# Two transformer blocks in fp32: another order of work in the first stage, and each head's pipeline step as one burst of TensorE

## The chip, the cores and the metric

One core of one Trainium2 chip runs the whole program. The metric is the device time of one execution in microseconds (us).

## The reference

Everything is fp32. A sequence of 256 tokens with 2048 channels goes through a first block and a second one. What the change touches lies in the first block, up to its attention's output:

```
h = rmsnorm(x, attn_norm)                  # (256, 2048)
proj = h @ w_in                            # (256, 5376)
aq, ak, av, bq, bk, bv, cq, ck, cv = split(proj)
out_a: 8 heads, windowed softmax, sinks, bias table (2 key/value heads)
out_b: 8 heads, stick-breaking: z = q k^T / 8, strictly causal,
       a = exp(log_sigmoid(z) + sum of log_sigmoid(-z) over the keys between)
out_c: 16 heads, softmax over three dilations, bias table
x = x + concat(rmsnorm(out_a), rmsnorm(out_b), rmsnorm(out_c)) @ w_out
```

A feed-forward part with a short convolution follows, then the second block (a pooling layer and a latent attention), which is steered by silu(c) @ ada_w, 12288 columns for each of two layers. Those ada products don't depend on x, and the kernel spreads them over its stages.

## The kernel before, in words

**Weights.** All weights pass through a ring of 4 slots (`raw`, `hi`, `lo`), in chunks of 512 KB: two tiles of 128 rows by 512 columns, or four by 256. SyncE loads a chunk (L943 to L949); it waits until the low half of the chunk four places before is made. ScalarE copies it to fp32r, the high half (`split_hi`, L540), once TensorE has used up the slot's last chunk; VectorE subtracts it from the raw values, the low half (`split_lo`, L544). TensorE multiplies three products (high x high, high x low, low x high), 12 matmuls of 512 columns a chunk (L630 in the first stage). So loads, high halves and low halves run ahead of TensorE by up to four places. An **ada chunk** goes through the same ring but not to TensorE: VectorE multiplies it by the two steering vectors and adds up, 4 instructions (L567, L573). When 8 are summed, TensorE turns the panel (`turn_ada`, L646) and VectorE takes it.

**The first stage** is a loop over c = 0 to 115, written out, that every engine runs in its own order; semaphores tie them. Chunks 0 to 83 are w_in in 11 panels (8 chunks each, panel 6 has 4), chunks 84 to 115 are w_out in 12. At the end of a panel ScalarE takes it out of PSUM (`take_in`, L1126), squares it for the head norms (L1133), VectorE sums the squares (`head_sums`, L1481), and GpSimd makes roots and stages q and k of each head. x itself is turned by TensorE (`turn_x`, L712) and split (`x_high` L725, `x_low` L735) at the start.

**The heads.** 32 heads, 8 "b" (stick-breaking), 8 "c", 8 "a", 8 "c", go through a pipeline of steps, called bursts. `BURST` names the chunk in front of which burst b stands: 19, 22, ... 40; 43, 45, 48, ... 60; 63, 65, ... 77; 79, 80, 82, 84 and so on to 102. At burst b:

- TensorE's `burst(b)`, in front of chunk BURST[b]: turn the mixed tile of two finished heads (L2030), turn q and k of head b (L1968), scores of head b-1 (L1978 to L1982).
- TensorE's `second_burst(b)`, in front of the chunk after it: for head b-3 the turn of the probabilities (L1992) or the stick sum (L2001, L2002), for head b-4 the output (L2019 to L2021). It waits for `exp_done` and `b_soft`, and for `pt_ready` and `b_weights`.
- ScalarE: q and k columns (L1141), the split of weights, then softmax exp (L1168); for every second "b" burst `stick_logs`, abs, exp and ln of a pair of heads (L1181 to L1185, table loads between), behind the weight split. `stick_weights` (L1190) stands at the start of the next chunk.
- VectorE: `soft_turned` and `stick_exponent` and `head_taken` one chunk later, logits and maxima (L1489 to L1500) in the burst's own chunk, then the low halves and ada chunks of that c, and last, one chunk later, `stick_soft` (L1513).

**Other work of the stage.** The position bias is made from 384 distances and a one-hot table (`bias_by_distance`, L1959), stored to DRAM, and read back by 8 transfers of 384 KB with rows of 1 KB (L964), all behind weight chunk 16. `FIRST_ADA` places two ada panels, 16 chunks, behind weight chunks 20, 23, ... 65; a weight or ada chunk is split about 3 to 4 places ahead of its turn. `FIRST_ADA_TURNS` places their turns at 47 and 72, in PSUM bank 7, which the heads' outputs use too, so the turn waits until the outputs are taken. The mean square of x is needed at the end of chunk 7 (`take_in(0)`).

Of the kernel before, what the change touches and what calls it, by code (L numbers as in the profile page):

```python
# [14 lines left out]
P = 128  # L15
# [22 lines left out]
W = 512  # L38
# [65 lines left out]
FIRST_ADA = [20 + 3 * m for m in range(2 * CH)]  # L104
FIRST_ADA_TURNS = [47, 72]
# [194 lines left out]
def two_block_kernel(nc, t, out, consts):  # L300
    ctx = ExitStack()
    with ctx:
# [625 lines left out]
        def _(sp):  # L928
# [30 lines left out]
            for j in range(RING, N_FIRST):  # L959
                load_first(j)  # L960
                if j == 2 * CH:
                    sp.wait_ge(bias_stored, 2 * 16)
                    for p in range(0, P, SHIFTS):
                        sp.dma_start(bias[p:p + SHIFTS, :, :],  # L964
                                     bass.AP(bias_rows.tensor, P - 1 - p, [[3 * P - 1, SHIFTS], [3 * P * SHIFTS, N_TAB], [1, SEQ]]))\
                          .then_inc(bias_loaded, 16)
                for m in range(len(FIRST_ADA)):
                    if first_at(j) + 1 <= FIRST_ORDER.index((True, m)) < first_at(j + 1):
                        c = FIRST_ORDER.index((True, m))
                        load_chunk(sp, c, c % RING, t["ada_w_2"][0][m % CH * CK_T * P:(m % CH + 1) * CK_T * P, m // CH * W:(m // CH + 1) * W], W)  # L970
# [125 lines left out]
        def _(act):  # L1096
# [15 lines left out]
            act.wait_ge(attn_ready, 1)  # L1112
            x_high(act, 0, 0)
            his(act, 0, 0, 0, 0, 2)
            x_high(act, 0, 1)
            his(act, 0, 0, 0, 2, RING)
            x_high(act, 0, 2)
            x_high(act, 0, 3)
# [73 lines left out]
            for c in range(N_FIRST):  # L1192
                for b in bursts_at(c - 1):
                    if headed(b, U_BEHIND, "b"):
                        stick_weights(headed(b, U_BEHIND, "b"))
                for b in bursts_at(c):
                    if b < HEADS:
                        qk_columns(heads[b])
                    if mix_pair(b) is not None:
                        mix_high(mix_pair(b))  # L1200
                if c in X_TURN_AT:
                    x_high(act, 1, X_TURN_AT.index(c))
                his(act, 0, 0, 0, first_at(c) + RING, first_at(c + 1) + RING)
                if c < D // W:
                    act.wait_ge(x_loaded[c], 16)
                    panel_squares(act, 0, c, x_squares[:, :])
# [15 lines left out]
                for b in bursts_at(c):  # L1222
                    if headed(b, S_BEHIND, "ac"):
                        soft_exp(headed(b, S_BEHIND, "ac"))
                    if headed(b, S_BEHIND, "b") and b % 2 == 0:
                        stick_logs(b // 2 - 1)
                    if mix_pair(b) is not None:
                        mix_square(mix_pair(b))
# [212 lines left out]
        def _(dve):  # L1441
# [10 lines left out]
            x_low(dve, 0, 0)  # L1452
            los(dve, 0, 0, 0, 0, 2)
            x_low(dve, 0, 1)
            los(dve, 0, 0, 0, 2, RING)
            x_low(dve, 0, 2)
            x_low(dve, 0, 3)
# [119 lines left out]
            for c in range(N_FIRST):  # L1577
# [3 lines left out]
                for b in bursts_at(c - 1):  # L1581
                    if headed(b, U_BEHIND, "ac"):
                        soft_turned(headed(b, U_BEHIND, "ac"))
                    if headed(b, U_BEHIND, "b"):
                        stick_exponent(headed(b, U_BEHIND, "b"))
                    if headed(b, V_BEHIND, "abc"):
                        head_taken(headed(b, V_BEHIND, "abc"))
                for b in bursts_at(c):
                    if headed(b, S_BEHIND, "ac"):
                        if b == HEADS_B + S_BEHIND:  # L1590
                            dve.wait_ge(bias_loaded, 16 * P // SHIFTS)
                        soft_logits(headed(b, S_BEHIND, "ac"))
                    if headed(b, S_BEHIND, "b"):
                        stick_logits(headed(b, S_BEHIND, "b"))
                    if headed(b, S_BEHIND + 1, "ac"):
                        soft_recip(headed(b, S_BEHIND + 1, "ac"))
                    if mix_pair(b) is not None:
                        mix_low(mix_pair(b))
# [6 lines left out]
                if c == RING:  # L1605
                    vector_columns()
                    x_mean_square(dve, 0)
                if c == CH - 2:
                    bias_rows_ready()
# [6 lines left out]
                for b in bursts_at(c - 1):  # L1616
                    if headed(b, S_BEHIND, "b") and b % 2 == 0:
                        stick_soft(b // 2 - 1)
# [322 lines left out]
        def _(pe):  # L1941
# [62 lines left out]
            def head_out(h):  # L2004
# [3 lines left out]
                for n, at in enumerate(FIRST_ADA_TURNS):  # L2008
                    if BURST[h.n + V_BEHIND] >= at:
# [76 lines left out]
            for c in range(N_FIRST):  # L2086
                if c in (1, 3):
                    pe.wait_ge(x_loaded[(c + 1) // 2], 16)
                    turn_x(pe, 0, (c + 1) // 2)
                if c == RING:  # L2090
                    pe.wait_ge(x_loaded[3], 16)
                    turn_x(pe, 0, 3)
# [4 lines left out]
                for b in bursts_at(c - 1):  # L2097
# [3 lines left out]
                if c in FIRST_ADA_TURNS:  # L2101
                    n = FIRST_ADA_TURNS.index(c)
                    pe.wait_ge(out_taken, sum(BURST[k + V_BEHIND] < c for k in range(HEADS)))
# [309 lines left out]
```

## Time and profile before

| | |
|---|---|
| runs | 2490.86, 2486.44, 2471.79 us; median 2486.44 |
| profiled execution | 2475.26 us, its span 2473.5 |
| TensorE busy | 95% of the span (2348.0 us) |
| VectorE, ScalarE, GpSimd busy | 67%, 42%, 3% |
| DMA | 430.32 MB, mean 174 GB/s |
| mean granted clock of TensorE | 0.98 of full speed |

A row of a timeline gives the start, the duration, the engine, the line of the kernel, the instruction with its operands, and, in brackets, how long its engine was idle before it and what ended that. Matmuls overlap, so what a chunk costs is read from the start of its first matmul to the start of what follows, not from durations. A busy share over the whole span hides that the first stage, until about 478 us, works differently from the rest.

### The profile page before, as it was taken

How to read it: one execution, taken by the hardware profiler on the slowest of the kernel's cores; microseconds unless marked ns; L12 is line 12 of the kernel's file. 1: busy time of each engine (PE TensorE's matmuls, PEld its weight loads, DVE VectorE, ACT ScalarE, POOL GpSimd, SP SyncE). 2: the span in 40 equal slices, each digit the busy share in tenths (PEclk: the TensorE clock that was granted, in tenths of full speed). 3: DMA queues.
4: the chain of work that ended last, by engine and by line, in shares of the span. 5: the costliest groups of instructions: out<-in, count | busy, mean ns of one | idle time of the engine just before them, and what ended most of it. 6: DMA issues, size and time to landing. Idle time of an engine off the chain costs nothing.

```text
span 2473.5 us, 32056 instructions
## 1 busy us (share of the span) xinstructions
PE 2348.0 (95%) x11221; PEld 1944.8 (79%) x11221; DVE 1658.1 (67%) x2401; ACT 1041.2 (42%) x1489; POOL 73.6 (3%) x112
## 2 busy tenths in 40 slices
PE   7889999999999999999979999999899799899998
PEld 6667778878788787777857888888788699799976
DVE  4466757677877877687757665757678666456644
ACT  5455655555555555434343222222322534444333
POOL 1011210000000000000000000000000000000000
PEclk9899999999999999999989999999999899999999
DMA  7855634566766767687754554646566256411243
GB/s 212 202 160 148 178 120 137 173 214 206 235 201 218 228 199 234 217 257 239 249 178 143 160 165 143 197 137 196 188 193 192 85 173 178 130 60 59 81 136 136
DMA packets 225515, 430.32 MB, mean 174 GB/s; under 512 B 13799, under 2 KB 38623, under 8 KB 224128
## 3 DMA queue, kind: packets, MB, share of 16 engines
q1 hardware_dynamic: 222112, 418.96, 54.8%
q10 hardware_dynamic: 2720, 9.83, 1.2%
q8 instruction: 63, 1.03, 0.2%
q14 instruction: 44, 0.36, 0.0%
q0 software_dynamic: 576, 0.14, 0.0%
HBM read 426.16 MB, written 2.72 MB: 173 GB/s over the span
## 4 chain that ended last, share of the span: by engine, by line
PE 61%; issue 19%; DVE 7%; DMA 6%; ACT 5%; SPq 0%; POOL 0%; DVEq 0%; ACTq 0%; POOLq 0%
PE ps L597 35%; PE ps L630 11%; PE ps L607 9%; DMA raw<-in_w_down 4%; DVE lo L544 2%; ACT hi L540 2%; DVE ada_acc L573 2%; PE ps L646 1%; DVE ustage L1633 1%; PE ps L2207 1%; DMA raw<-in_ada_w 1%; DMA raw<-in_w_in 1%; PE ps L2132 0%; SPq L964 0%; PE ps L1982 0%
## 5 line engine op out<-in xcount | busy, mean ns | idle before, releaser
L540 ACT ACTIVATE hi<-raw 128x1024 fp32r<-128x1024 f32 x604 | 634.6, 1059 | 1169.9 <-PE ps L597 528.8
L544 DVE TENSOR_TENSOR lo<-raw,hi 128x1024 fp32r<-128x1024 f32 x604 | 731.8, 1223 | 546.5 <-ACT hi L540 540.3
L573 DVE SCALAR_TENSOR_TENSOR ada_acc<-raw,csil,ada_acc 128x512 f32<-128x512 f32 x720 | 491.8, 748 | 2.7 <-DMA raw<-in_ada_w 2.5
L597 PE MATMUL ps<-hi,h_hi 128*128 128x512 f32 x960 | 383.9, 400 | 8.1 <-DVE lo L544 6.6
L597 PE MATMUL ps<-lo,h_hi 128*128 128x512 f32 x960 | 379.4, 395 | 0.0
L597 PE MATMUL ps<-hi,h_lo 128*128 128x512 f32 x960 | 379.3, 395 | 0.0
L597 PEld LDWEIGHTS ps<-hi,h_hi 128*128 128x128 f32 x960 | 181.2, 189 | 55.7 <-DVE lo L544 13.5
L597 PEld LDWEIGHTS ps<-hi,h_lo 128*128 128x128 f32 x960 | 181.2, 189 | 42.4
L597 PEld LDWEIGHTS ps<-lo,h_hi 128*128 128x128 f32 x960 | 181.3, 189 | 40.2
L630 PE MATMUL ps<-hi,h_hi 128*128 128x512 f32 (+1 forms) x352 | 146.1, 415 | 19.9 <-DVE lo L544 19.9
L597 PE MATMUL ps<-hi,g_hi 128*128 128x512 f32 x352 | 140.9, 400 | 3.0 <-DVE lo L544 2.7
L630 PE MATMUL ps<-lo,h_hi 128*128 128x512 f32 (+1 forms) x352 | 139.7, 397 | 0.0
L597 PE MATMUL ps<-lo,g_hi 128*128 128x512 f32 x352 | 139.6, 397 | 0.0
L597 PE MATMUL ps<-hi,g_lo 128*128 128x512 f32 x352 | 139.4, 396 | 0.0
L630 PE MATMUL ps<-hi,h_lo 128*128 128x512 f32 (+1 forms) x352 | 139.2, 396 | 0.0
L597 PE MATMUL ps<-hi,k_hi 128*128 128x448 f32 (+2 forms) x288 | 102.6, 356 | 1.1 <-DVE k_lo L836 0.6
L597 PE MATMUL ps<-hi,y_hi 128*128 128x512 f32 x256 | 102.5, 400 | 0.0
L630 PEld LDWEIGHTS ps<-hi,h_hi 128*128 128x128 f32 x352 | 69.6, 198 | 41.5 <-issue 15.6
L607 PE MATMUL ps<-h_hi,hi 128*128 128x512 f32 x256 | 102.0, 398 | 0.0
L597 PE MATMUL ps<-hi,y_lo 128*128 128x512 f32 x256 | 101.9, 398 | 0.0
L597 PE MATMUL ps<-lo,y_hi 128*128 128x512 f32 x256 | 101.9, 398 | 0.0
L597 PE MATMUL ps<-hi,k_lo 128*128 128x448 f32 (+2 forms) x288 | 101.5, 353 | 0.0
(319 smaller groups left out, 3751.2 us busy)
## 6 DMA issues: line engine op xcount, KB each, us to landing
raw<-in_ada_w SPq DMA_DIRECT2D x192, 512.0 KB, 4.2
raw<-in_w_up SPq DMA_DIRECT2D x176, 512.0 KB, 4.4
raw<-in_w_down SPq DMA_DIRECT2D x88, 512.0 KB, 5.1
raw<-in_w_in SPq DMA_DIRECT2D x84, 512.0 KB, 4.0
raw<-in_pool_w_in SPq DMA_DIRECT2D x64, 512.0 KB, 4.0
raw<-in_mla_w_in SPq DMA_DIRECT2D x56, 448.0 KB, 4.1
raw<-in_w_out SPq DMA_DIRECT2D x32, 512.0 KB, 3.8
raw<-in_pool_w_out SPq DMA_DIRECT2D x32, 512.0 KB, 4.6
```

What stands on the lines that cost most here:

```text
L540: act.activation(hi[:, slot, :, :], raw[:, slot, :, :], ACT.Copy).then_inc(hi_split, 1 + ada)
L544: dve.tensor_tensor(lo[:, slot, :, :], raw[:, slot, :, :], hi[:, slot, :, :].bitcast(F32), ALU.subtract).then_inc(lo_split, 1)
L573: ins = dve.scalar_tensor_tensor(acc, raw[:, slot, k, :], csil[:, v, kt:kt + 1], acc, ALU.mult, ALU.add)
L597: mm = pe.matmul(ps[:, bank, 0:n], a[:, kt0 + k, tok * P:(tok + 1) * P], w[:, slot, k, col0:col0 + n], start=first and k == 0 and s == 0, ...
L607: mm = pe.matmul(ps[:, bank0 + n, :], w[:, slot, k, n * P:(n + 1) * P], a[:, kt0 + k, :], start=first and k == 0 and s == 0, stop=last and ...
L630: mm = pe.matmul(ps[:, PAIR * half + tok, 0:width], x, w[:, k, :], start=first and k == 0 and s == 0, stop=last and k == nk - 1 and s == 2)
L646: mm = pe.matmul(ps[:, bank, at:at + 1], acc, negones[:, 0:1], start=True, stop=True)
L1633: ins = dve.scalar_tensor_tensor(conv[which][:, m, back:SEQ], turned_u(m)[:, 0:SEQ - back], cols[:, bass.ds(ch + vec[0] * P + vec[1], 1)], ...
L2207: mm = pe.matmul(ps[:, m, s * SEQ + c0:(s + 1) * SEQ], u[:, TT * s + k, m * P:(m + 1) * P], poolm[:, bass.ds(n, 1), k, c0:].rearrange("p a ...
```

## The change

- **One burst.** `second_burst(b)` and VectorE's items of it stand at BURST[b] itself, in front of `burst(b)`, no longer one chunk later. `stick_weights` follows in the same chunk, behind the split of weights.
- **Logs first.** `stick_logs` stands in front of ScalarE's split of weights, `stick_soft` in front of VectorE's logits and splits of the next chunk.
- **The start.** ScalarE does a small activation as soon as its operand is set, then splits weight chunk 0 before x's first part, and so on in turns; VectorE does the same. TensorE turns x panels 1 and 2 in front of chunk 1, panel 3 in front of chunk 2. The squares of x move from chunks 0 to 3 to chunks 2 to 5, its mean from 4 to 6.
- **The bias loads** go one by one behind weight loads 20, 22, ... 34.
- **The ada chunks** go behind weight chunks 40, 42, 45, 47, ... 77, their turns to 62 and 83, and bank 7's order follows.

```diff
--- before.py
+++ after.py
@@ -101,8 +101,9 @@
          + [79 + 23 * k // 12 for k in range(N_BURSTS - 24)])
 QK_READY = {0: IN_AT[2], 8: IN_AT[5], 16: IN_AT[8], 24: IN_AT[10]}
 STAGE_AT = [max(BURST[max(k - PAIR, 0)] if k >= PAIR else 0, QK_READY[k // 8 * 8]) for k in range(HEADS)]
-FIRST_ADA = [20 + 3 * m for m in range(2 * CH)]
-FIRST_ADA_TURNS = [47, 72]
+FIRST_ADA = [40 + 5 * m // 2 for m in range(2 * CH)]
+FIRST_ADA_TURNS = [62, 83]
+BIAS_AT = range(20, 36, 2)
 GROUP_MEAN_AT = [BURST[12] + 1, BURST[28] + 1, BURST[36] + 1]
 X_TURN_AT = [OUT_AT[8 + n + 1] + 1 for n in range(D // W - 1)]
 UP_PAIRS = 2
@@ -958,12 +959,12 @@
             load_x(3)
             for j in range(RING, N_FIRST):
                 load_first(j)
-                if j == 2 * CH:
+                if j in BIAS_AT:
+                    p = BIAS_AT.index(j) * SHIFTS
                     sp.wait_ge(bias_stored, 2 * 16)
-                    for p in range(0, P, SHIFTS):
-                        sp.dma_start(bias[p:p + SHIFTS, :, :],
-                                     bass.AP(bias_rows.tensor, P - 1 - p, [[3 * P - 1, SHIFTS], [3 * P * SHIFTS, N_TAB], [1, SEQ]]))\
-                          .then_inc(bias_loaded, 16)
+                    sp.dma_start(bias[p:p + SHIFTS, :, :],
+                                 bass.AP(bias_rows.tensor, P - 1 - p, [[3 * P - 1, SHIFTS], [3 * P * SHIFTS, N_TAB], [1, SEQ]]))\
+                      .then_inc(bias_loaded, 16)
                 for m in range(len(FIRST_ADA)):
                     if first_at(j) + 1 <= FIRST_ORDER.index((True, m)) < first_at(j + 1):
                         c = FIRST_ORDER.index((True, m))
@@ -1109,13 +1110,13 @@
             act.sem_inc(mla_taken, PAIR)
             for s in (x_squared, u_staged[0], u_staged[1], g_hi_done):
                 act.sem_inc(s, FREE)
-            act.wait_ge(attn_ready, 1)
-            x_high(act, 0, 0)
-            his(act, 0, 0, 0, 0, 2)
-            x_high(act, 0, 1)
-            his(act, 0, 0, 0, 2, RING)
-            x_high(act, 0, 2)
-            x_high(act, 0, 3)
+            act.wait_ge(consts_set, 1)
+            act.activation(x_squares[:, 0:TT], halves[:, 0:TT], ACT.Identity)
+            for n in range(D // W):
+                his(act, 0, 0, 0, n, n + 1)
+                if n == 0:
+                    act.wait_ge(attn_ready, 1)
+                x_high(act, 0, n)
 
             def take_in(p):
 
@@ -1190,20 +1191,22 @@
                 act.activation(stick_one(b_w, h), stick_one(b_z, h), ACT.Exp).then_inc(b_weights, 1)
 
             for c in range(N_FIRST):
-                for b in bursts_at(c - 1):
-                    if headed(b, U_BEHIND, "b"):
-                        stick_weights(headed(b, U_BEHIND, "b"))
                 for b in bursts_at(c):
                     if b < HEADS:
                         qk_columns(heads[b])
                     if mix_pair(b) is not None:
                         mix_high(mix_pair(b))
+                    if headed(b, S_BEHIND, "b") and b % 2 == 0:
+                        stick_logs(b // 2 - 1)
                 if c in X_TURN_AT:
                     x_high(act, 1, X_TURN_AT.index(c))
                 his(act, 0, 0, 0, first_at(c) + RING, first_at(c + 1) + RING)
-                if c < D // W:
-                    act.wait_ge(x_loaded[c], 16)
-                    panel_squares(act, 0, c, x_squares[:, :])
+                for b in bursts_at(c):
+                    if headed(b, U_BEHIND, "b"):
+                        stick_weights(headed(b, U_BEHIND, "b"))
+                if c in range(2, 2 + D // W):
+                    act.wait_ge(x_loaded[c - 2], 16)
+                    panel_squares(act, 0, c - 2, x_squares[:, :])
                 if c == CH - 2:
                     act.wait_ge(ext_ready, 2)
                     for to, e, n in ((0, 0, HEADS_A), (HEADS_A, 1, HEADS_C)):
@@ -1222,8 +1225,6 @@
                 for b in bursts_at(c):
                     if headed(b, S_BEHIND, "ac"):
                         soft_exp(headed(b, S_BEHIND, "ac"))
-                    if headed(b, S_BEHIND, "b") and b % 2 == 0:
-                        stick_logs(b // 2 - 1)
                     if mix_pair(b) is not None:
                         mix_square(mix_pair(b))
                 if c + 1 in X_TURN_AT or c + 1 == N_FIRST:
@@ -1449,12 +1450,9 @@
             dve.memset(table[N_BUCKETS:N_BUCKETS + 1, :], 1.0).then_inc(consts_set, 1)
             dve.wait_ge(attn_turned, 1)
             dve.tensor_copy(attn_col[:, :], ps[:, 0, 0:KT]).then_inc(attn_ready, 1)
-            x_low(dve, 0, 0)
-            los(dve, 0, 0, 0, 0, 2)
-            x_low(dve, 0, 1)
-            los(dve, 0, 0, 0, 2, RING)
-            x_low(dve, 0, 2)
-            x_low(dve, 0, 3)
+            for n in range(D // W):
+                los(dve, 0, 0, 0, n, n + 1)
+                x_low(dve, 0, n)
 
             def vector_columns():
 
@@ -1578,13 +1576,16 @@
                 for p in HSS_OF:
                     if IN_AT[p + 1] == c:
                         head_sums(p)
-                for b in bursts_at(c - 1):
+                for b in bursts_at(c):
                     if headed(b, U_BEHIND, "ac"):
                         soft_turned(headed(b, U_BEHIND, "ac"))
                     if headed(b, U_BEHIND, "b"):
                         stick_exponent(headed(b, U_BEHIND, "b"))
                     if headed(b, V_BEHIND, "abc"):
                         head_taken(headed(b, V_BEHIND, "abc"))
+                for b in bursts_at(c - 1):
+                    if headed(b, S_BEHIND, "b") and b % 2 == 0:
+                        stick_soft(b // 2 - 1)
                 for b in bursts_at(c):
                     if headed(b, S_BEHIND, "ac"):
                         if b == HEADS_B + S_BEHIND:
@@ -1604,8 +1605,8 @@
                     group_mean(GROUP_MEAN_AT.index(c))
                 if c == RING:
                     vector_columns()
+                if c == CH - 2:
                     x_mean_square(dve, 0)
-                if c == CH - 2:
                     bias_rows_ready()
                 if c == FIRST_ADA[0]:
                     dve.wait_ge(c_silu, 1)
@@ -1613,9 +1614,6 @@
                     if OUT_AT[q + 1] == c + 1:
                         add_out(q)
                 los(dve, 0, 0, 0, first_at(c) + RING, first_at(c + 1) + RING)
-                for b in bursts_at(c - 1):
-                    if headed(b, S_BEHIND, "b") and b % 2 == 0:
-                        stick_soft(b // 2 - 1)
 
             def add_panel(done, c, half, col0):
 
@@ -2006,7 +2004,7 @@
                 if h.n:
                     pe.wait_ge(out_taken, h.n)
                 for n, at in enumerate(FIRST_ADA_TURNS):
-                    if BURST[h.n + V_BEHIND] >= at:
+                    if BURST[h.n + V_BEHIND] > at:
                         pe.wait_ge(ada_taken, n + 1 + FREE)
                 pe.wait_ge(proj_taken, h.v_panel + 1)
                 if h.kind == "b":
@@ -2084,23 +2082,21 @@
             pe.wait_ge(x_loaded[0], 16)
             turn_x(pe, 0, 0)
             for c in range(N_FIRST):
-                if c in (1, 3):
-                    pe.wait_ge(x_loaded[(c + 1) // 2], 16)
-                    turn_x(pe, 0, (c + 1) // 2)
+                for n in {1: (1, 2), 2: (3,)}.get(c, ()):
+                    pe.wait_ge(x_loaded[n], 16)
+                    turn_x(pe, 0, n)
                 if c == RING:
-                    pe.wait_ge(x_loaded[3], 16)
-                    turn_x(pe, 0, 3)
                     pe.wait_ge(attn_ready, 1)
                     turn_vectors()
                 if c == CH - 2:
                     bias_by_distance()
-                for b in bursts_at(c - 1):
+                for b in bursts_at(c):
                     second_burst(b)
                 for b in bursts_at(c):
                     burst(b)
                 if c in FIRST_ADA_TURNS:
                     n = FIRST_ADA_TURNS.index(c)
-                    pe.wait_ge(out_taken, sum(BURST[k + V_BEHIND] < c for k in range(HEADS)))
+                    pe.wait_ge(out_taken, sum(BURST[k + V_BEHIND] <= c for k in range(HEADS)))
                     pe.wait_ge(lo_split, FIRST_ORDER.index((True, n * CH + CH - 1)) + RING + 1)
                     turn_ada(pe, n, (n % PAIR,), 7)
                 if c in X_TURN_AT:
```

## Rows read from the trace of the kernel before

**Rows 1.** what TensorE waited for, 0 to 480 us: total, times, longest

```profile
PE ps L630 <- DVE lo L544: 19.9, 4, 11.8
PE ps L2001 <- DVE b_w L1513: 13.4, 4, 4.9
...
PE ps L646 <- DVE mixed L1548: 2.2, 1, 2.2
```

**Rows 2.** two stretches; us, busy per engine (count), clock, DMA share, GB/s

```profile
80.00:100.00 20.00, 15.52 (x56) 12.42 (x57) 9.47 (x10) 9.06 (x11) 1.52 (x6) 0.74 0.75 243
323.60:356.80 33.20, 33.20 (x168) 25.84 (x167) 22.68 (x54) 22.15 (x56) 7.92 (x12) 1.00 0.41 122
```

**Rows 3.** TensorE in time: start us, us, line, names, [idle before <-releaser]

```profile
101.51 0.38 PE L1968 MATMUL ps<-ident,stage 128*128 128x128 f32 x2
...
102.67 0.50 PE L630 MATMUL ps<-hi,h_hi 128*128 128x512 f32 x1
...
111.14 0.27 PE L1968 MATMUL ps<-ident,stage 128*128 128x128 f32 x1
...
351.76 0.49 PE L1992 MATMUL ps<-ident,probs 128*128 128x128 f32 x3
...
353.87 0.50 PE L630 MATMUL ps<-hi,h_hi 128*128 128x512 f32 x1
...
372.65 0.49 PE L1992 MATMUL ps<-ident,probs 128*128 128x128 f32 x3
...
373.57 0.47 PE L630 MATMUL ps<-hi,mix_b_hi 128*128 128x512 f32 x1
...
376.44 0.38 PE L2030 MATMUL ps<-ident,mixed 128*128 128x128 f32 x2
```

**Rows 4.** ScalarE and TensorE in time, start of the program to head 0

```profile
7.29 1.28 ACT L725 ACT_TABLE_LOAD   x1 [7.29 <-PE ps L712]
...
12.50 0.77 PE L630 MATMUL ps<-hi,h_hi 128*128 128x512 f32 x1 [4.45 <-DVE lo L544]
...
32.34 0.65 PE L630 MATMUL ps<-hi,h_hi 128*128 128x512 f32 x1 [2.86 <-DVE lo L544]
...
40.21 0.48 PE L1959 MATMUL ps<-onehot,table 33*8 33x384 f32 x1 [0.50 <-DVE cols L1463]
...
41.59 0.50 PE L630 MATMUL ps<-hi,h_hi 128*128 128x512 f32 x1
...
92.89 0.38 PE L1968 MATMUL ps<-ident,stage 128*128 128x128 f32 x2
```

**Rows 5.** the page's costliest groups: busy us, mean ns | idle before

```profile
L540 ACT ACTIVATE hi<-raw 128x1024 fp32r<-128x1024 f32 x604 | 634.6, 1059 | 1169.9 <-PE ps L597 528.8
L544 DVE TENSOR_TENSOR lo<-raw,hi 128x1024 fp32r<-128x1024 f32 x604 | 731.8, 1223 | 546.5 <-ACT hi L540 540.3
L573 DVE SCALAR_TENSOR_TENSOR ada_acc<-raw,csil,ada_acc 128x512 f32<-128x512 f32 x720 | 491.8, 748 | 2.7 <-DMA raw<-in_ada_w 2.5
```

**Rows 6.** transfers of 5 to 17.5 us, then of 58 to 80 us

```profile
DMA packets 3376, 4.57 MB, mean 366 GB/s; under 512 B 763, under 2 KB 1321, under 8 KB 3376
DMA packets 3317, 3.50 MB, mean 159 GB/s; under 512 B 138, under 2 KB 3090, under 8 KB 3316
```

**Rows 7.** the stick pairs: groups of ScalarE, then VectorE and TensorE in time

```profile
L1185 ACT ACT_TABLE_LOAD x4 | 5.1, 1283 | 0.1
...
L1185 ACT ACTIVATE b_w<-b_w 128x768 f32<-128x768 f32 x4 | 3.4, 845 | 0.0
...
143.41 1.23 DVE L1481 TENSOR_REDUCE hss<-ps 128x16 f32<-128x1024 f32 x1 [1.34 <-ACT ps L1133]
...
154.79 0.59 PE L2001 MATMUL ps<-b_w,stick 128*128 128x384 f32 x1 [3.97 <-DVE b_w L1513]
```

**Rows 8.** TensorE behind the second ada turn

```profile
319.15 0.75 PE L630 MATMUL ps<-hi,h_hi 128*128 128x512 f32 x1
...
323.58 0.38 PE L1968 MATMUL ps<-ident,stage 128*128 128x128 f32 x2
```

## The prediction

> **What bounds the kernel now.** I read the waits of TensorE first, then the times at which its chunks start, then what ended each wait. In the first stage TensorE loses time in three kinds of waits [rows 1]: 19.9 us in 4 waits for a low half of weights, 13.4 us in 4 waits for a stick-breaking operand, 2.2 us for a head's output in front of the turn of an ada panel. Behind them the granted clock falls: 0.74 in the mean of 80 to 100 us [rows 2], where full is 1.00. When nothing is late, three chunks take 8.47 us (102.67 to 111.14), 2.82 us each, a chunk alone 2.87, a first burst 1.16, a second burst 0.92 [rows 3]. The stage's floor is thus TensorE's own work, and what can be won is waits, the low clock behind them, and joints. Everything after the stage is untouched; I cost it at nothing.
>
> **The start.** Before, the activation table is loaded at 7.29 us, in front of the first high half of x, and costs 1.28 us there; the first chunk starts at 12.50 [rows 4]. After, the dummy activation loads it while the first transfers run, and weight chunk 0 is split before x; one of the two splits that stood in the chain (L540, 1.06 us [rows 5]) leaves it partly. I take 10.8 for the first chunk. From there: chunk 0 at the low clock about 4 us; the turns of panels 1 and 2 together about 1.6 us and about 1 us until x panel 2 has landed (my estimate from its place behind 3.7 MB at 366 GB/s [rows 6]); chunk 1, one turn, chunks 2 and 3, the vectors: 2.8 + 0.8 + 5.7 + 0.8. Chunk 4 starts at 27.6 to 27.9, where it started at 32.34: 4.5 us. Chunks 4 and 5, with a wait of 0.5 for the bias matmuls, took 32.34 to 40.21 = 7.87 us [rows 4]; at full clock they take 5.7, 2.2 us more. The squares, which move to chunks 2 to 5, fill ScalarE there, but its weight splits stay three chunks ahead. Sum **-6.7**; bounds -3 (transfers set the order) and -8.5. The Trainium skill (ScalarE: Activation LUTs, What ACT_TABLE_LOAD costs) puts a switch of table at about 2.66 us, a drain included. By that the moved load would be worth 1.4 us more; here the row shows 1.28, and the activation follows at once, so the trace decides against it.
>
> **The bias loads.** Chunks 6 to 18, 13 of them, take 41.59 to 92.89 = 51.3 us [rows 4]; at 2.82 they take 36.7. The difference is the 11.8 us wait and the clock behind it [rows 1, 2]. Eight issues of 384 KB ran in one piece at 159 GB/s against 366 GB/s for the weights [rows 6], and the weight chunks stood behind them: 3.1 MB, 20 us. Spread over j = 20 to 34, one costs 0.39 MB / 159 = 2.5 us of DMA per two chunks, the two weight chunks 2 x 0.52 / 366 = 2.9: 5.4 us in a period of 5.6 (before the first head) to 8. It fits narrowly, and no ada chunk is loaded there any more. A chunk's load is issued about 9 us before ScalarE wants it, and low halves are three chunks ahead, so a delay of 2.5 us hides. SyncE's wait for the stored rows comes with load 20, long after the store. I keep 0.6 us for contention: **-14**; bounds -15 and -5.
>
> **The stick-breaking heads.** Four pairs of heads, four waits [rows 1]. The chain of a pair is logits (VectorE), abs, exp, ln (3 x 0.85 and a table load of 1.28 [rows 7]) on ScalarE, the softplus on VectorE, the sum on TensorE. The logs now stand before the split of weights and the softplus before the softmax and the next splits; but the sum comes one chunk earlier. Counted from the start of the burst at which the logs are made (T), VectorE ends the previous low half at T+2.6, the logits are there at T+3.9, the logs at T+7.8 (pair 0, with a second table load but no second burst before it: T+8.3). Then come a high half, its low half (1.06 and 1.23 [rows 5]) and the softplus (about 0.95). Pair 0: T+11.5 against a need at 1.16 + 3 x 2.82 = T+9.6: waits 1.9. Pair 1 has chunk 31's end of panel 3 in between: before the softplus VectorE takes the head sums, which wait for ScalarE's take-in and squares [rows 7]; T+15.3 against T+11.1: waits 4.2, where it waited 3.97 [rows 7]. Pair 2 has no weight split between: no wait. Pair 3 is at burst 43, the next is at 45, and an ada chunk (4 x 0.75 us [rows 5]) is ahead of its logits: T+13.8 against T+8.5: waits 5.3. Together 11.4 for 13.4: 2 us. A long wait also costs some 1.6 us in the chunk behind it (4.43 us for 2.87 [rows 8]) and up to 1 in its own burst; one such tail goes, one shrinks: 3.5. Sum **-5.5**; bounds -20 (all four go) and +8 (each grows by an ada chunk's 3).
>
> **The turns of ada panels.** The turn at 72 stood one burst behind a head's output and waited 2.2 us for VectorE, and the clock fell: chunk 4.43 us [rows 1, 8]. At 62 and 83 the last output is one or two chunks old, and VectorE takes it in time. -2.2 - 1.6 and 0.9 for slow turns: **-4.7**; bounds -5 and 0. The wait of the next head's output for the turned panel loses its equal sign; nothing else waits.
>
> **The merged bursts.** One pair is merged in the trace already (79 and 80): 2.11 us, against 0.92 + 1.16 apart [rows 3]: +0.03. One run of chunks less is broken: 2.87 against 2.82, -0.05, up to -0.1 for both sides. With 36 second bursts **-1.8**; bounds 0 and -3.
>
> **VectorE from 60 to 75.** Before, no ada chunk met the "a" heads' two-chunk rhythm; from 323.6 to 356.8 us VectorE is busy 22.7 of 33.2 us over eight chunks, 2.8 each [rows 2]. Now 7 ada chunks of 3 us fall on 16 chunks: 1.3 more, 4.1 of about 4.1. By items: a burst's T+2.6 grows to T+5 behind an ada chunk, the logits are ready at T+6.5, and the next burst needs them at T+8: hidden, with 1.5 to spare. Where head sums come too (60, 76) it is about 0. I take **+2**, since a full queue must slip somewhere; bounds 0 and +50.
>
> **Sum**: -6.7 - 14 - 5.5 - 4.7 - 1.8 + 2 = -31. The profiled execution took 2475.26 us (span 2473.5), which gives 2444. The median of the three runs is 2486.44, 11 above it; by that it is 2455. I say 2450.
>
> **Rivals.** (a) *All stick waits go*, because the softplus is ready whenever logs come before the split. For it: logs and softplus both move forward. Against it: pairs 1 and 3 above. The 11.4 us and their tails, 17 together, go too: 2433. Chance 0.12.
> (b) *The bias loads still collide.* For it: 5.4 of 5.6 us. Each weight chunk would land late, and half of the 51.3 - 36.7 comes back, with little from the start: gain 10 to 25, 2468. Chance 0.14. (c) *Only the two large terms halve each* for reasons that I do not see: 2467, chance 0.07.
> (d) *Slower: VectorE becomes the bound.* Its place is the 16 bursts from 43 to 77; an ada chunk in front of the softmax items makes the next burst wait. It decides once the wait and its low-clock tail are above 31 / 16 = 2 us a burst. With 2.2 us of wait and 1.55 of tail it costs 60, 29 slower: 2515. For it: the count above leaves nothing free. Against it: ada chunks only meet four bursts in ten, and a merged step lets the queue catch up for a chunk. Chance 0.08, half of it slower by over 1%.
> (e) *The merged bursts cool the array.* In the trace a merged burst of 2.11 us is followed by a chunk at its usual pace, and the granted clock of 323.6 to 356.8 us, which holds it, is 1.00 [rows 2, 3]. If it fell each time, 36 times some 1.6 us (57 us) would be paid, 26 more than the gain: 2512. Chance 0.03. The Trainium skill (TensorE: Matmul & The Clock Gate, Part 4: PE-mode transpose) says that transposes do not count as busy for the clock gate; by that rule this rival would be likely, and the trace so far does not bear it out.
>
> **Chances.** Forecast 0.56, (a) 0.12, (b) 0.14, (c) 0.07, (d) 0.08, (e) 0.03. A measurement of this kernel tells about 1% (25 us) from no change. Faster by more: 0.56 + 0.12, less a little for the forecast's lower edge, 0.66. Within: 0.25. Slower: 0.09. The range from 2428 (a, with the start's best) to 2478 (b, and an edge of d) leaves out 2 in 10.
>
> **What would show it.** Right: no wait above 2 us between chunks 6 and 18, and head 0's turn near 72 us where it was at 92.89; three waits at the stick sum of about 2, 4 and 5 us, none at the third pair; no wait at the ada turns; merged bursts of 2.1 to 2.8 us with chunks of 2.82 to 2.9 behind them; VectorE above 90% in chunks 60 to 75. Wrong: a weight chunk landing late between chunks 12 and 26, waits of TensorE for logits or turned probabilities in the second half, or a clock below 1.00 behind merged bursts.

## The result and the profile after

Over seven runs of each, the changed kernel takes 2456.73 us in the median (2451.76 to 2461.12), the kernel before 2484.17 (2471.79 to 2490.86). The ratio is 0.9891, with a 95% interval of 0.9867 to 0.9915: faster by 1.1%, 27.4 us. The profiled execution of the changed kernel took 2456.73 us, too (span 2454.9), 18.5 less than the profiled one of before. Both numbers are needed below, where the 9 us between them are taken up.

First the waits of TensorE in the first stage (0 to 480 us): line waited at, releaser, us in total, times, longest.

```profile
PE ps L1999 <- DVE b_w L1511: 14.9, 3, 6.0
PE ps L2081 <- DMA attn_rows<-in_attn_norm: 5.9, 1, 5.9
PE ps L631 <- DVE h_lo L736: 2.9, 1, 2.9
PE ps L1966 <- POOL stage L1062: 1.2, 1, 1.2
```

Against [rows 1] the waits for a low half of weights and for the mixed heads are gone. The 5.9 us are the wait for the first data of the program, and the 2.9 us come right behind it. The waits at the stick-breaking sum have become fewer, three for four, but their sum has grown from 13.4 to 14.9 us.

Then the start and the first heads, from TensorE in time (start us, us, line, names, idle before with its releaser).

```profile
11.00 0.79 PE L631 MATMUL ps<-hi,h_hi 128*128 128x512 f32 x1 [2.87 <-DVE h_lo L736]
...
28.08 0.48 PE L631 MATMUL ps<-hi,h_hi 128*128 128x512 f32 x1
...
35.22 0.50 PE L631 MATMUL ps<-hi,h_hi 128*128 128x512 f32 x1
...
71.58 0.27 PE L1966 MATMUL ps<-ident,stage 128*128 128x128 f32 x1
```

These rows answer to [rows 4]. Chunk 0 starts at 11.00 (12.50 before), chunk 4 at 28.08 (32.34), chunk 6 at 35.22 (41.59), and head 0's turn is at 71.58 (92.89). Chunks 6 to 18 take 36.36 us where they took 51.3.

Next the stick pairs: what waited, and how the burst and the run of chunks behind it went, in the same view.

```profile
105.63 1.01 PE L1999 MATMUL ps<-b_w,stick 128*128 128x384 f32 x1 [6.04 <-DVE b_w L1511]
...
109.64 0.79 PE L631 MATMUL ps<-hi,h_hi 128*128 128x512 f32 x1
...
119.34 0.81 PE L1999 MATMUL ps<-b_w,stick 128*128 128x384 f32 x2
...
121.98 0.50 PE L631 MATMUL ps<-hi,h_hi 128*128 128x512 f32 x1
...
134.48 1.65 PE L1999 MATMUL ps<-b_w,stick 128*128 128x384 f32 x2 [3.84 <-DVE b_w L1511]
...
139.66 0.79 PE L631 MATMUL ps<-hi,h_hi 128*128 128x512 f32 x1
...
149.68 0.48 PE L1999 MATMUL ps<-b_w,stick 128*128 128x384 f32 x1
...
185.87 1.01 PE L1999 MATMUL ps<-b_w,stick 128*128 128x384 f32 x1 [5.00 <-DVE b_w L1511]
```

A merged stick burst that waits for nothing takes 121.98 - 119.34 = 2.64 us. The one behind the wait of 3.84 us takes 139.66 - 134.48 = 5.18, and the three chunks behind it 10.02 instead of 8.47. So the wait is paid twice over: 3.84, and 2.54 + 1.55 = 4.09 in its tail. The first pair's tail (a burst of 4.01, three chunks of 9.70) and the last one's (5.19, and 9.92) are alike. Before, the second bursts stood alone behind the same waits; their four tails sum to 7.6 us, the three of now to 11.2 (each is what the burst and the chunks up to the next burst take beyond their undisturbed 2.64, or 1.46 alone, and 2.82 to 2.89 a chunk; pair 0's burst has no outputs and is 2.13, or 0.97 alone). The bursts' part of these sums went from 3.0 to 7.0 us, that of the chunks from 4.6 to 4.2.

Over the length of the burst at 134.48 the granted clock is at its lower level, 0.50 (1.2 of 2.4 GHz). The second row is the same burst behind the same wait in run 6 below, where it takes 4.40 us: there the clock is back at 1.00 before the burst ends. Columns as in the stretches further down.

```profile
134.40:139.60 5.20, 5.12 (x16) 3.84 (x16) 3.09 (x5) 0.76 (x2) 4.35 (x4) 0.50 0.53 156
132.20:136.60 4.40, 4.37 (x16) 3.32 (x16) 3.05 (x4) 0.69 (x2) 4.31 (x4) 0.61 0.47 140
```

The second half of the stage, in the same view.

```profile
254.79 1.84 PE L647 MATMUL ps<-ident,ada_acc 128*128 128x1 f32 x16
256.49 0.48 PE L631 MATMUL ps<-hi,h_hi 128*128 128x512 f32 x1
...
315.08 0.49 PE L1990 MATMUL ps<-ident,probs 128*128 128x128 f32 x3
...
317.19 0.51 PE L631 MATMUL ps<-hi,h_hi 128*128 128x512 f32 x1
...
325.38 0.33 PE L1966 MATMUL ps<-ident,stage 128*128 128x128 f32 x1 [1.16 <-POOL stage L1062]
...
457.50 0.39 PE L598 MATMUL ps<-hi,h_hi 128*128 128x512 f32 x1
```

An ada turn is 1.70 us with no wait. The 5.10 us of before, from 314.05 to 319.15, were a second burst (0.92), a wait of 2.19 and a slow turn, and a chunk of 4.43 stood behind them [rows 8]. A merged burst without a stick operand is 2.11 us, and its chunks keep their pace. The stage ends at 457.50 (477.77 before): 20.3 us earlier. What follows takes 1995.7 us before and 1997.4 now.

Last the clock, from three stretches: us, busy us (and count) of PE, weight loads, VectorE, ScalarE, GpSimd, then granted clock, DMA share, GB/s.

```profile
90.00:152.00 62.00, 52.12 (x207) 40.34 (x206) 23.52 (x27) 33.89 (x43) 7.20 (x10) 0.83 0.62 147
105.00:200.00 95.00, 85.53 (x346) 66.62 (x347) 49.11 (x68) 52.81 (x78) 15.97 (x18) 0.85 0.48 134
247.00:307.00 60.00, 59.98 (x308) 48.07 (x307) 52.02 (x102) 36.71 (x87) 19.97 (x20) 1.00 0.58 178
```

The stick heads run at 0.85; the dense stretch of merged bursts and ada chunks at 1.00, with VectorE busy 52.02 of 60 us and TensorE waiting for nothing.

### The profile page after: what moved, and what is told of

Same layout as the page of the kernel before. It is cut to its first block, busy times and chain, and to the rows that moved or that the text cites. A ratio compares the mean times of both kernels' runs of the same rounds, so it can differ in the third digit from the quotient of the medians.

```text
span 2454.9 us, 32050 instructions
## 1 busy us (share of the span) xinstructions
PE 2347.2 (96%) x11221; PEld 1943.8 (79%) x11221; DVE 1658.4 (68%) x2401; ACT 1041.6 (42%) x1490; POOL 86.6 (4%) x112
## 4 chain that ended last, share of the span: by engine, by line
PE 62%; issue 19%; DVE 8%; DMA 6%; ACT 4%; POOL 0%; DVEq 0%; ACTq 0%; SPq 0%; POOLq 0%
PE ps L598 36%; PE ps L631 11%; PE ps L608 9%; DMA raw<-in_w_down 4%; DVE lo L545 2%; ACT hi L541 2%; DVE ada_acc L574 2%; PE ps L647 1%; DVE ustage L1631 1%; DMA raw<-in_w_in 1%; PE ps L2203 1%; PE ps L2128 0%; PE ps L1980 0%; PE ps L775 0%; PE ps L1979 0%
## 5 line engine op out<-in xcount | busy, mean ns | idle before, releaser
L598 PEld LDWEIGHTS ps<-hi,h_hi 128*128 128x128 f32 x960 | 181.2, 189 | 55.4 <-DVE lo L545 13.3
L598 PE MATMUL ps<-lo,k_hi 128*128 128x448 f32 (+2 forms) x288 | 101.5, 352 | 0.0
```

Of the source, the lines that this page charges most:

```text
L598: mm = pe.matmul(ps[:, bank, 0:n], a[:, kt0 + k, tok * P:(tok + 1) * P], w[:, slot, k, col0:col0 + n], start=first and k == 0 and s == 0, ...
```

## The experiments

**Runs 1 to 4: one part at a time.** They tell how the gain divides, and whether the merge is one of its parts at all. First the new order of the start alone, on the kernel before.

```diff
-            x_high(act, 0, 0)
-            his(act, 0, 0, 0, 0, 2)
...
+            act.activation(x_squares[:, 0:TT], halves[:, 0:TT], ACT.Identity)
+            for n in range(D // W):
+                his(act, 0, 0, 0, n, n + 1)
...
+                for n in {1: (1, 2), 2: (3,)}.get(c, ()):
```

> The kernel before with the start alone (dummy activation, weights and x split in turns, squares and mean two chunks later). My theory: the first matmul of a chunk starts about 1.5 us earlier, chunk 6 about 6 us earlier than 41.6, and the wait of 11.8 us behind the bias loads stays as it is, since the stored bias rows come earlier too: 6 us less in all, 0.25%. Rival: what the start gives, the wait behind the bias loads takes back, and the time is the same.

Measured: 2472.79 us against 2480.30, 0.9967 (0.9954 to 0.9980). Chunk 6 starts at 35.19, as in the changed kernel. But its bias loads, which are not changed, cost more than in the profile of before:

```profile
84.36 0.79 PE L630 MATMUL ps<-hi,h_hi 128*128 128x512 f32 x1 [18.22 <-DVE lo L544]
```

TensorE waits 18.22 us in one place where it waited 11.8 [rows 1], and the 13 chunks take 56.7 us for 51.3. That row is of TensorE in time. To see whether the stall comes from the new start, the kernel before was profiled once more, unchanged:

> The kernel before, once more, for another profiled execution. My theory: the 13 chunks from number 6 took 51.3 us in the first profile, with a wait of 11.8, but 56.6 to 56.7, with a wait of 18.2, in the two experiments that keep the bias loads in one piece; that stretch varies from execution to execution, and it is why the first profiled execution lay 9 us under the median. So here the stretch takes either about 51 or about 57 us, and the rest of the stage agrees within 1 us with the first profile. Rival: the variation lies elsewhere, and this stretch takes 51.3 again.

The waits of TensorE, 0 to 480 us,

```profile
PE ps L630 <- DVE lo L544: 22.0, 4, 13.9
PE ps L2001 <- DVE b_w L1513: 13.3, 4, 4.9
```

and the first row's longest wait in time:

```profile
86.58 0.80 PE L630 MATMUL ps<-hi,h_hi 128*128 128x512 f32 x1 [13.90 <-DVE lo L544]
```

Here it waits 13.90 us, and the execution took 2475.97 us. The 13 chunks take 52.4 us, nearer to the first profile's 51.3 than to 56.7, so the long stall was not seen in this kernel itself. The same program thus has a bias stall that differs by 2.1 us between two executions, and the third run below, with a start as before, has 18.2. The other waits stay as they are (13.3 and 13.4 at the stick sum), but their tails do not: the four sum to 6.8 us where they were 7.6, and the slow stretch at the second ada turn is 1.4 us longer.

Second, the spread bias loads with the ada chunks and turns at their new places, the rest as before.

```diff
+FIRST_ADA = [40 + 5 * m // 2 for m in range(2 * CH)]
+FIRST_ADA_TURNS = [62, 83]
+BIAS_AT = range(20, 36, 2)
...
-                if j == 2 * CH:
+                if j in BIAS_AT:
```

> The kernel before with the bias loads spread over weight loads 20 to 34 and the ada chunks and their turns placed later; start, logs and bursts as before. My theory: 13 chunks from number 6 take about 36.5 us instead of 51.3 (15 less); the turn at 72 loses its wait and tail (4 less); the stick pairs 0 to 2 lose the ada chunk in front of the softplus, but pair 0 gets late weights from the bias loads, so the waits of 13.4 us become 7 to 11: 21 to 25 us less in all. Rival (the bias loads only move their cost to the weights of chunks 20 to 26): 10 us less or nothing.

Measured: 2463.57 us against 2480.30, 0.9931 (0.9915 to 0.9947), 17 us faster. The waits of TensorE up to 480 us:

```profile
PE ps L2002 <- DVE b_w L1514: 10.2, 3, 6.1
PE ps L631 <- DVE lo L545: 8.1, 3, 4.4
...
PE ps L647 <- DVE mixed L1549: 5.1, 2, 3.0
PE ps L2031 <- DVE mixed L1549: 2.5, 3, 1.1
```

The bias stall is gone (the 8.1 us are those of the start), and the 13 chunks take 36.36. What is missing against the expected 21 to 25 stands in the last two rows: with second bursts of their own, both turns at their new places wait for a head's output, 5.1 us in all for 2.2, the mixed heads wait 2.5 us for 0.5, and the waits have tails. The new places are good ones only with the merge.

Third, the merge alone: on TensorE, as in the lines shown, and with it VectorE's items and the stick weights.

```diff
-                for b in bursts_at(c - 1):
+                for b in bursts_at(c):
                     second_burst(b)
```

> The kernel before with the bursts merged alone: second bursts, VectorE's items and the stick weights at the burst's own chunk; logs behind the split, softplus last, bias loads, ada chunks and start as before. My theory: the stick sum is needed one chunk earlier while its operand is no earlier, so each of the four waits grows by about 2.9 us and its slow burst by 1: 12 to 16 us more. Rival (what the merge is for): 36 joints less, 0.04 to 0.1 us each, 1.5 to 3.5 us less.

Measured: 2500.34 us against 2480.30, 1.0077 (1.0062 to 1.0093), 20 us slower. TensorE's waits:

```profile
PE ps L2001 <- DVE b_w L1513: 29.8, 4, 9.0
PE ps L630 <- DVE lo L544: 26.3, 4, 18.2
```

The waits at the stick sum grow from 13.4 to 29.8 us, since the sum stands a chunk earlier behind the same chain; the four bursts behind them lose 9.5 us, where the single ones of before lost 3.0. That is more than the 12 to 16 us expected. There is no wait at the ada turns. Alone, the merge is a loss.

Fourth, the changed kernel with the merge undone on all three engines, so that second bursts come a chunk later again.

```diff
-                for b in bursts_at(c):
+                for b in bursts_at(c - 1):
                     second_burst(b)
```

> The changed kernel with the merge alone undone: second bursts one chunk later on TensorE, VectorE and for the stick weights; all else as changed. My theory: the waits of 6.0, 3.8 and 5.0 us at the stick sums shrink by a chunk each to about 3.1, 0.9 and 2.1, with smaller tails, against 1.5 us for the joints: 10 to 12 us faster than the changed kernel, about 2445. Rival: the merge pays, and this is 1 to 4 us slower than the changed kernel.

Measured: 2445.03 us against 2480.30, 0.9869 (0.9847 to 0.9891). That is 12 us below the changed kernel's median, but the kernel before was 4 us faster beside it, too: by the ratios, 0.9869 and 0.9891, it is 5 us, with intervals that overlap. The profiles say more: the stage ends at 445.03, 12.5 us earlier than in the changed kernel. TensorE's waits:

```profile
PE ps L647 <- DVE mixed L1546: 5.1, 2, 3.0
...
PE ps L2028 <- DVE mixed L1546: 2.5, 3, 1.1
PE ps L1999 <- DVE b_w L1511: 2.2, 2, 1.4
```

The earlier logs and softplus do what they can when the sum leaves them time: 2.2 us of wait, where run 2, without them, has 10.2 and the kernel before 13.4. With the merge in place the sum is a chunk earlier, and the wait is 14.9. The merge costs 12.7 us of wait there, and wins back the two turns' 5.1 and the mixed heads' 2.5; the tails make the rest.

**Runs 5 to 7: each stick wait by itself.** Three waits remain, and each was given a cause of its own: pair 0 late weights, pair 1 the head sums in front of the softplus, pair 3 an ada chunk in front of the logits. The reason for the first is in what ScalarE waits for between 60 and 110 us in the changed kernel (total, times, longest), and in one of its rows in time:

```profile
ACT hi L541 <- DMA raw<-in_w_in: 17.9, 7, 4.0
ACT hi L541 <- PE ps L631: 4.0, 3, 1.7
```

```profile
92.29 1.06 ACT L541 ACTIVATE hi<-raw 128x1024 fp32r<-128x1024 f32 x1 [3.49 <-DMA raw<-in_w_in]
```

ScalarE waits for weights there, seven times, and the transfers of 69 to 97 us have a mean of 208 GB/s with the DMA engines full throughout. TensorE does not notice, three chunks ahead as the split is; but the logits of pair 0 on VectorE, and with them the logs, queue behind a split that is late. Run 5 spreads the bias loads further.

```diff
-BIAS_AT = range(20, 36, 2)
+BIAS_AT = range(20, 44, 3)
```

> The changed kernel with the eight bias loads behind weight loads 20, 23, ... 41 instead of 20, 22, ... 34. My theory: the weights of chunks 20 to 29 land late because of the bias loads between them, and that holds the logs of stick pair 0; with more room no high half waits for a transfer by more than 1 us, the wait at pair 0 falls from 6.0 us to about 2, and the whole to 4 to 7 us less. Rival: the wait is the chain of the logs itself, moved before the split, and stays at 6.

The same waits of ScalarE, and then those of TensorE up to 480 us:

```profile
ACT hi L541 <- DMA raw<-in_w_in: 4.0, 2, 2.6
```

```profile
PE ps L1999 <- DVE b_w L1511: 11.5, 3, 5.0
...
PE ps L1966 <- POOL stage L1062: 1.2, 1, 1.2
```

Measured: 2449.55 us against 2483.07, 0.9867 (0.9838 to 0.9897). ScalarE's waits for weights fall from 17.9 to 4.0 us and pair 0's wait from 6.04 to 2.62; the other two stay at 3.86 and 5.00. Run 6 moves the ada chunks out of the way of pair 3.

```diff
-FIRST_ADA = [40 + 5 * m // 2 for m in range(2 * CH)]
+FIRST_ADA = [46 + 2 * m for m in range(2 * CH)]
```

> The changed kernel with the ada chunks behind weight chunks 46, 48, ... 76. My theory: no ada chunk is then in front of the logits of stick pair 3, and no high half between its logs and its softplus, so its wait of 5.0 us falls to about 0.3 and the slow clock behind it goes: 7 to 9 us less. At one ada chunk in two weight chunks VectorE is fuller in chunks 46 to 75 than before: up to 3 us of that can come back. Rival (VectorE is the bound there): as slow as the changed kernel or slower, with new waits from chunk 55 on.

TensorE's waits in it:

```profile
PE ps L1999 <- DVE b_w L1511: 9.3, 2, 5.5
...
PE ps L1966 <- DVE mix_lo L1552: 0.7, 1, 0.7
```

Measured: 2443.78 us against 2483.07, 0.9849 (0.9825 to 0.9874). Pair 3's wait is gone (5.48 and 3.86 stay), and so is the one for GpSimd's stage; a new one of 0.7 us has come. In its profiled execution the stage ends 15.8 us earlier, which is more than the wait of 5.0 with a tail of 4.0 and the other one's 2.9; most of the rest is that the tails of pairs 0 and 1 are shorter here, 3.5 us together for 7.2 (bursts of 3.84 and 4.40, with three chunks of 8.47 behind them). Why the clock came back sooner in them was not found out. Run 7 puts the softplus in front of the head sums.

```diff
             for c in range(N_FIRST):
+                for b in bursts_at(c - 1):
+                    if headed(b, S_BEHIND, "b") and b % 2 == 0:
+                        stick_soft(b // 2 - 1)
                 for p in HSS_OF:
```

> The changed kernel with VectorE's softplus of a stick pair in front of the head sums of the same chunk. My theory: the wait at pair 1 (3.8 us) is the head sums' wait for ScalarE's take-in and squares; it falls to 0.5 or less, its slow burst and chunks go with it: 5 to 8 us less. Rival (the logs on ScalarE are late by themselves): the wait stays above 3 us.

TensorE's waits at the stick sum:

```profile
PE ps L1999 <- DVE b_w L1511: 10.1, 2, 5.1
```

Measured: 2446.81 us against 2483.07, 0.9864 (0.9838 to 0.9890). Pair 1's wait is gone; 5.15 and 5.00 stay. Each cause is thus shown by an edit that takes away its wait and leaves the other two in place, within a microsecond.

**Runs 8 to 10: all three edits together,** with the merge, without it, and with a merge from the thirteenth burst on. The middle one undoes the merge as run 4 did; the last one has this line and reads second bursts from it.

```diff
+SECOND = [at + (k < 12) for k, at in enumerate(BURST)]
```

> The changed kernel with the three single edits together: bias loads behind every third weight load, ada chunks from 46 on, softplus in front of the head sums. My theory: each edit removes its own wait (pair 0 to 2.6 us, pair 3 and pair 1 to about 0), and they add up: 7 + 13 + 10 = 30 us less than the changed kernel, about 2427. Rival (a wait removed lets the next one out, so that the sum is less): 2435 or more.

> As the kernel with the three edits together, but with every second burst back at the next chunk. My theory: the stick sums wait for nothing, 4 to 5 us less than with the three edits merged; but the ada turns at 62 and 83 then stand one chunk or less behind a head's output (5.1 us of waits in the experiment that undid the merge alone), and turns of mixed tiles wait 2.5, with slow clock behind, 8 to 10 us more: about 2432. Rival (the merge only costs): 2422 or less.

> The three edits together, second bursts one chunk later for bursts 0 to 11 (all that a stick-breaking head needs), merged from burst 12 on. My theory: both gains at once, the stick sums wait for nothing and the ada turns neither: 4 to 6 us less than the three edits merged throughout, about 2422, the fastest of all. Rival (the merge point makes no difference once the three edits are in): within 2 us of the three edits merged.

All three against 2484.28 us. Merged: 2432.03 (2423.36 to 2433.61), 0.9786 (0.9757 to 0.9814). Not merged: 2441.84, 0.9836 (0.9810 to 0.9862). Merged from the thirteenth burst on: 2430.86 (2427.88 to 2432.86), 0.9789 (0.9762 to 0.9815). The rows are the waits of the merged kernel (without those of the program's first 11 us) and its stretch of the stick heads, then the waits of the one that is not merged.

```profile
PE ps L1999 <- DVE b_w L1511: 1.6, 1, 1.6
PE ps L1966 <- DVE mix_lo L1552: 0.7, 1, 0.7
```

```profile
105.00:200.00 95.00, 95.00 (x500) 77.90 (x499) 61.14 (x94) 65.79 (x108) 20.85 (x24) 1.00 0.60 168
```

```profile
PE ps L647 <- DVE mixed L1546: 4.6, 2, 2.4
...
PE ps L2028 <- DVE mixed L1546: 2.0, 2, 1.2
```

The stretch from 105 to 200 us now has TensorE busy all the time at a clock of 1.00, where it was 0.85. And the sign of the merge has turned: alone it cost 20 us (run 3) and in the changed kernel 5 to 12 (run 4), and behind the three edits it gives 10 us. Its price was the stick waits and their tails, which are gone but for 1.6 us, and its gain, the waits at the turns and mixed heads, is left. In run 8's profiled execution the stage ends 27.6 us earlier than in the changed kernel and the execution only 23.1; why what follows takes 4.5 us longer there was not found out. Run 8 comes 5 us short of its forecast of 2427, run 9 is 10 us slower than forecast, and run 10 comes out as its rival says. Keeping the early second bursts apart as well takes the last 1.6 us of wait away and gains nothing that can be told from no change. The kernel with the three edits beats both kernels of this case, by 2.1% the one before and, comparing the ratios, by some 1% the changed one.

## Why the prediction was right, and where it was not

The median of 2456.73 is 7 above the predicted 2450 and inside the range; a gain of more than 1% was the likeliest case. The steps, on the profiled pair:

- **The start** (-6.7): chunk 6 starts 6.4 us earlier. The size is right. The table load hides less than was said: it starts at 6.45, only 0.84 us before the old 7.29, and the rest of the 1.5 us that chunk 0 gains comes from the split of weights (1.06) that left the chain.
- **The bias loads** (-14): the 13 chunks take 14.9 less, and all of the stall and its tail went. Right for TensorE. The contention was not as harmless as I took it to be. I counted a weight load as issued 9 us before ScalarE wants it; from 69 to 97 us the median from issue to landing is 11.4 us. Weights came late to ScalarE, and that was paid at the stick sum.
- **The stick-breaking heads** (-5.5): this is the step that failed. The waits were forecast as 1.9, 4.2, none and 5.3, and are 6.04, 3.84, none and 5.00. Three of four are right, by the causes that were named; pair 0 was counted with weights on time, and run 5 brings it down to 2.62 once they nearly are. With it the waits grow by 1.5 us where 2 less was forecast. The larger part of the miss is the tails, 3.5 less in the forecast and 3.6 more in the trace (7.6 to 11.2). I had let one tail go and one shrink, and left out that the merged burst, 2.64 us long, now stands right behind the wait, so that twice as much burst runs at the low clock: the chunks' part of the tails did not grow, the bursts' part did (3.0 to 7.0), and run 3, where the merge is the only change, has 9.5. How soon the clock comes back differs between profiles, though: in run 6 the waits at pairs 0 and 1 (5.48 and 3.86) have tails of 1.7 and 1.8 us for 3.1 and 4.1, so some of the growth may belong to this execution. The term is +5.1, 10.6 us off.
- **The turns of ada panels** (-4.7): both take 1.70 with no wait, -4.0 (2.5 at the turn, 1.55 in the chunk behind it). The wait and the chunk are as forecast, and the slow turn itself lost 0.3 and not 0.9. Right; runs 2, 4 and 9 show that they owe it to the merge.
- **The merged bursts** (-1.8): 2.11 for 0.92 + 1.16, and a run of two chunks 5.68 to 5.70 for two of about 2.88, about -0.04 for each, -1.5 in all. The term is right as joints. But the prediction asked of the merge only what it does to joints, and its weight was elsewhere: 12.7 us of wait at the stick sum.
- **VectorE** (+2): busy 87% of 247 to 307 us, not above 90%, and TensorE waits for nothing there. One wait of 1.16 us at 325.38, for a head's stage on GpSimd, costs 2.9 with its tail. GpSimd is late because VectorE's head sums of chunk 76 start at 317.71, behind an ada chunk and a split, where ScalarE's squares were done at 316.04; the prediction had given that place about 0 to spare. In run 6, with the ada chunks elsewhere, this wait is gone. The size is right.

These sum to -18.8 (6.4 + 14.9 + 4.0 + 1.5 = 26.8, less 5.1 and 2.9). Two small waits of before, 0.65 us for a stage at 277.40 and 0.49 for a mixed head at 293.78, cost 1.5 us with what stands around them and are gone too. The stage ends 20.3 earlier. Against -31 nearly all of the difference is the stick step. So 2444 on the profiled execution was 13 too low, 10.7 of it in the stage.

That the median came out closer than that is luck. Of the 11 us between the profiled execution of before and its median I carried 6 over to the changed kernel, from 2444 to 2450, and its profiled execution lies at its median. The 11 us were no constant. The bias stall of the old order was 11.8 us in the profiled execution, 13.9 in another of the same kernel, and 18.2 in two kernels that still had that order; the change removes it however long it is, and the stretch is 36.36 in the changed kernel and in run 2 alike. If the longer stall is the usual one, a typical execution before thus had more to win than the profiled one. Chunks 6 to 18 took 56.7 us with the longer stall, 5.4 more than in the profiled execution. That is the larger part of the 9 us between -18.5 and -27.4, if the timed executions of before had the stall as long as runs 1 and 3. Run 1 speaks for it: its profiled execution, with the stall of 18.2, took 2473.21 us where its median is 2472.79. But no execution of the kernel before at its median was profiled, so this part, and the rest, is argued and not shown. Two errors, one of 13 us and one of 6 in the other direction, stand behind 2450, and leave the 7 us by which it is off.

Of the rivals, (b) was half right: the bias loads still collide with weights, but TensorE pays 3.4 us at the stick sum, by run 5, and not 10 or more at the weights. (a) describes the kernel of run 8, where nearly all stick waits are gone. Its time of 2432 is close to the 2433 worked out for (a), by chance: the waits and tails of the changed kernel were 26 us and not 17, and 2433 was counted from 2450. For (c) the prediction shows no working that gives 2467: half of the two large terms is 10 us. (d) and (e) did not come about: with merged bursts and ada chunks the granted clock of 247 to 307 us is 1.00.

By the rule that transposes do not count as busy (the Trainium skill, TensorE: Matmul & The Clock Gate, Part 4: PE-mode transpose), bursts in which half of the matmuls or more are transposes might have brought the clock down. The trace does not bear that out. No clock below 1.00 appears in that stretch, nor a slow chunk behind a burst that had not waited.

## What to carry to other kernels

When a step is moved earlier, the chain that feeds it is what to price, from its slowest input on: the same merge cost 20 us alone and gave 10 us in the end, and what turned it was the order of three items on VectorE and ScalarE, the places of the bias loads, and those of the ada chunks. Price a wait of TensorE with what stands behind it, since what follows at once runs at the low clock; put a long burst there and the tail grows with it. And look at what the profiled execution may hide by luck: a stall behind a crowded DMA queue can be half as long again in the next one.

## What the runs showed of the hardware

- Behind waits of 3.8 to 6.0 us of TensorE, with the granted clock at 0.83 over 90 to 152 us, a burst with the three chunks after it loses 3.1 to 4.1 us. One of 2.62 us (run 5) costs the same 3.1 as one of 6.04. Behind those of 5.48 and 3.86 us in run 6 it loses 1.7 and 1.8, and one of 1.57 us (run 8) leaves the stretch behind it at 1.00, while one of 1.16 us (325.38) cost 1.8 us in its tail. The length of a wait alone does not tell whether there is a tail.
- Eight loads of 384 KB in one piece stall TensorE for 11.8, 13.9, 18.2 and 18.2 us in four profiled executions whose orders there are the same. Spread out, the stretch is 36.35 to 36.50 us in nine profiles.
- With the bias loads spread, the two kinds of transfers move 208 GB/s together (69 to 97 us) where 5 to 17.5 us had 366 GB/s [rows 6]: enough for TensorE, and late for ScalarE seven times.
